# Values from three row tiles on, x of the second half loaded in one go, and mixed operands held in four PSUM banks, in a one-core encoder block

## What is computed

```python
h = rms_norm(x)
proj = h @ w_in            # lru_u | lru_y | q | k | v | gate_lru | gate_attn
lru_out = rg_lru(conv(lru_u)) * gelu(lru_y)       # 1280 channels, a scan over rows
attn_out = sliding_window_attention(q, k, v)      # 16 heads, 4 kv heads, 128 rows
mix = (g_lru * (lru_out @ w_lru_br) + g_attn * (attn_out @ w_attn_br)) @ w_out
x = x + rms_norm(mix)
h = rms_norm(x)
f = (silu(h @ w_ffn_gate) * (h @ w_ffn_up)) @ w_ffn_down
x = x + rms_norm(f)
```

## Time and profile before

| | |
|---|---|
| median of 3 runs | 1664.21 us (1663.47 to 1666.27) |
| the profiled execution | 1664.01 us, span 1662.2 us from first to last instruction |
| granted TensorE clock, mean | 0.99 of 2.4 GHz |
| PE busy | 1620.5 us, 97% of the span |
| POOL busy | 1231.1 us, 74% |
| DVE busy | 914.0 us, 55% |
| ACT busy | 571.3 us, 34% |
| moved by DMA | 187.88 MB, mean 113 GB/s |

### The profile page before, as it was taken

The page is one execution under the profiler, slowest core; times in us unless marked ns, Lnnn a source line. Parts: engine busy times, 40 slices in busy tenths (PEclk is TensorE's granted clock), DMA queues, the critical chain, the costliest instruction groups (busy, mean ns, idle before and its releaser), DMA issues.

```text
span 1662.2 us, 24258 instructions
## 1 busy us (share of the span) xinstructions
PE 1620.5 (97%) x7396; PEld 1337.0 (80%) x7396; DVE 914.0 (55%) x1160; ACT 571.3 (34%) x1073; POOL 1231.1 (74%) x1306
## 2 busy tenths in 40 slices
PE   8999999999999999999999998899999999999998
PEld 6788788888888888888878877688888888788887
DVE  5666536652265656666532457987775558415502
ACT  4588434532225776254422243310000113102101
POOL 5677767677786777777777876688887778768875
PEclk8999999999999999999999999999999999999999
DMA  4444433233354443522333564244432221633642
GB/s 149 121 114 115 111 97 90 80 92 95 95 146 123 115 120 99 163 81 74 89 95 95 147 218 154 75 121 115 114 95 64 68 76 57 236 97 95 221 121 86
DMA packets 119411, 187.88 MB, mean 113 GB/s; under 512 B 13345, under 2 KB 44321, under 8 KB 119329
## 3 DMA queue, kind: packets, MB, share of 16 engines
q1 hardware_dynamic: 95712, 143.18, 31.4%
q10 hardware_dynamic: 23616, 43.66, 8.0%
HBM read 162.93 MB, written 17.56 MB: 109 GB/s over the span
## 4 chain that ended last, share of the span: by engine, by line
PE 87%; DVE 6%; ACT 2%; issue 2%; DMA 1%; POOL 1%; ACTq 0%; DVEq 0%; POOLq 0%; SPq 0%
PE ps L818 14%; PE ps L819 14%; PE ps L817 14%; PE ps L1052 7%; PE ps L1054 7%; PE ps L1053 7%; PE ps L1146 4%; PE ps L1147 4%; PE ps L1148 4%; DMA xs<-x_t 1%; PE ps L871 1%; PE ps L872 1%; PE ps L873 1%; PE ps L888 1%; PE ps L967 1%
## 5 line engine op out<-in xcount | busy, mean ns | idle before, releaser
L660 POOL TENSOR_TENSOR w_lo<-w_raw,w_hi 128x512 fp32r<-128x512 f32 (+2 forms) x374 | 452.0, 1209 | 31.2
L657 POOL TENSOR_SCALAR w_hi<-w_raw 128x512 fp32r<-128x512 f32 (+2 forms) x374 | 240.2, 642 | 210.5 <-PE ps L819 130.0
L817 PE MATMUL ps<-h_hi,w_hi 128*128 128x512 f32 x672 | 263.7, 392 | 2.7 <-DVE g_h L1854 1.5
L818 PE MATMUL ps<-h_lo,w_hi 128*128 128x512 f32 x672 | 264.7, 394 | 0.0
L819 PE MATMUL ps<-h_hi,w_lo 128*128 128x512 f32 x672 | 264.1, 393 | 0.0
L817 PEld LDWEIGHTS ps<-h_hi,w_hi 128*128 128x128 f32 x672 | 126.5, 188 | 31.3 <-issue 1.8
L818 PEld LDWEIGHTS ps<-h_lo,w_hi 128*128 128x128 f32 x672 | 126.5, 188 | 27.2
L819 PEld LDWEIGHTS ps<-h_hi,w_lo 128*128 128x128 f32 x672 | 126.5, 188 | 27.2
L1798 DVE TENSOR_TENSOR acc<-acc,sq 128x512 f32<-128x512 f32 x47 | 49.3, 1049 | 175.3 <-ACT sq L1522 163.0
L1052 PE MATMUL ps<-t,w_hi 128*128 128x512 f32 x352 | 138.7, 394 | 1.4 <-POOL w_lo L710 1.4
L1054 PE MATMUL ps<-t,w_lo 128*128 128x512 f32 x352 | 138.0, 392 | 0.0
(11 more groups left out here) (363 smaller groups left out, 4054.0 us busy)
## 6 DMA issues: line engine op xcount, KB each, us to landing
w_raw<-w_f SPq DMA_DIRECT2D x68, 256.0 KB, 3.2
w_raw<-w_step SPq DMA_DIRECT2D x64, 256.0 KB, 2.7
w_raw<-w_b SPq DMA_DIRECT2D x64, 256.0 KB, 3.1
w_raw<-w_d SPq DMA_DIRECT2D x64, 256.0 KB, 2.7
w_raw<-w_a SPq DMA_DIRECT2D x96, 128.0 KB, 2.0
xs<-x_t ACTq DMA_DIRECT2D x32, 256.0 KB, 3.6
w_raw<-w_q SPq DMA_DIRECT2D x32, 256.0 KB, 3.1
w_raw<-w_o SPq DMA_DIRECT2D x32, 256.0 KB, 3.1
```

The lines of the kernel that those rows point to most:

```text
L657: nc.gpsimd.tensor_scalar(w_hi[:, s, w], w_raw[:, s, w], 1.0, 0.0, ALU.mult, ALU.add).then_inc(w_hi_made, 1)
L660: nc.gpsimd.tensor_tensor(w_lo[:, s, w], w_raw[:, s, w], rd(w_hi[:, s, w]), ALU.subtract).then_inc(w_lo_made, 1)
L817: mm(out, w_hi[:, s, w], x_hi, start=(k == 0), stop=False)
L818: mm(out, w_hi[:, s, w], x_lo, start=False, stop=False)
```

## The change

**Values.** PE waits for eight scans only and multiplies row tiles 0 to 2 with the first two weight blocks; then it waits for the ninth scan and multiplies row tile 3 with these two blocks, then all four tiles with blocks 2 and 3. The wait for the tenth scan moves behind the first tile of Q.

**x of the second half.** A buffer `x_next` of eight tiles lies on the place of b22. `between` of the second half issues its eight loads on ACT, after `normed_stream`. The loads in `x1_row` go, and `add_row` reads `x_next`; DVE waits once for all eight.

**Mixed operands.** Banks 4 to 7 (`BK_T`) take the first four tiles of h and then t1, the base of t2 and t4 in place; t3 and the last four tiles of h stay in SBUF. ACT copies t2's base to `rows` (`t2_keep`). The order on DVE and ACT is new, `stat_sum(5)` comes one pair of products earlier (t == 5), the weights of column tile 1 are loaded at t == 6 in place of t == 9, and `first_two` waits for each bank's low part of t4.

```diff
+        x_next = at("x_next", [P, KD, T], F32, reg_b + 4 * quad)
...
+        BK_INV, BK_ROW, BK_SQ, BK_T = 7, 5, (4, 6), (4, 5, 6, 7)
...
-                if t == 9:
+                if t == 6:
+                    sp_eng.wait_ge(normed, 3 * KD)
                     load_a21(1)
                     load_a12(1)
-                    sp_eng.wait_ge(added, 2 * KD)
                     load_a22(1)
                     load_a11(1)
...
+                pe.wait_ge(scanned, KR * h + 8)
+                pe.wait_ge(k_lo_made, PAIRS * h + 1)
+
+                def values(b, m):
...
+                for b in range(2):
+                    pe.wait_ge(w_lo_made, n_v + b + 1)
+                    for m in range(3):
+                        values(b, m)
                 pe.wait_ge(scanned, KR * h + 9)
-                pe.wait_ge(k_lo_made, PAIRS * h + 1)
-                for b in range(4):
+                for b in range(2):
+                    values(b, 3).then_inc(blocks_done, 1)
+                for b in range(2, 4):
                     pe.wait_ge(w_lo_made, n_v + b + 1)
...
+                    for m in range(3):
+                        values(b, m)
+                    values(b, 3).then_inc(blocks_done, 1)
...
+                project(0, n_q, 0, UNIT, h_hi, h_lo)
                 pe.wait_ge(scanned, KR * (h + 1))
-                for t in range(2):
-                    project(t, n_q + 2 * t, 2 * t, UNIT, h_hi, h_lo)
+                project(1, n_q + 2, 2, UNIT, h_hi, h_lo)
...
-                    if t == 6:
+                    if t == 5:
                         stat_sum(5)
...
-                    rows_out(n, o, 2, lambda: normed_stream(2, 3, x1_d[0]))
+
+                    def between():
+                        normed_stream(2, 3, x1_d[0])
+                        for c in range(KD):
+                            act.dma_start(x_next[:, c, :], x_d[1][c]).then_inc(x_next_loaded, 16)
+                    rows_out(n, o, 2, between)
...
+            def t2_keep(k):
+                act.wait_ge(t2_made, k + 1)
+                fn(rows[:, k, :], ps[:, BK_T[k], :], ACT.Copy).then_inc(t2_kept, 1)
...
-                dve.wait_ge(xs_loaded[c % 2], 16 * (4 * 4 + c // 2 + 1))
-                tt(rows[:, c, :], ps[:, 5, :], xs[:, c % 2, :], ALU.add).then_inc(added, 1)
+                tt(rows[:, c, :], ps[:, BK_ROW, :], x_next[:, c, :], ALU.add).then_inc(added, 1)
```

More of the change, by code:

```diff
@@ L919, in kvq @@
                 pe.wait_ge(dev_made, 3 if h else 1)
+                pe.wait_ge(scanned, KR * h + 8)
+                pe.wait_ge(k_lo_made, PAIRS * h + 1)
+                def values(b, m):
+                    out, t = ps[:, BK_V[m], 0:D_KV], slice(m * P, (m + 1) * P)
+                    for q in range(2):
+                        k, w = 2 * b + q, slice(q * D_KV, (q + 1) * D_KV)
+                        mm(out, h_hi[:, k, t], w_hi[:, b, w], start=(k == 0), stop=False)
+                        mm(out, h_lo[:, k, t], w_hi[:, b, w], start=False, stop=False)
+                        last = mm(out, h_hi[:, k, t], w_lo[:, b, w], start=False, stop=(k == KD - 1))
+                    return last
@@ L1661, in _ @@
             x1_row(1)
+            x1_row(2)
             first_copy(3)
-            x1_row(2)
+            x1_row(3)
             second_copy(2)
-            x1_row(3)
+            x1_row(4)
             first_copy(4)
-            x1_row(4)
+            x1_row(5)
+            x1_row(6)
             second_copy(3)
-            x1_row(5)
+            x1_row(7)
             first_copy(5)
-            x1_row(6)
+            acc_hi(5)
             second_copy(4)
-            x1_row(7)
-            acc_hi(5)
+            deviation(5)
             first_copy(6)
             second_copy(5)
-            deviation(5)
             first_copy(7)
+            for k in range(K2):
+                t_hi(h1_made, b22, rows[:, K2 + k, :], k)
             second_copy(6)
+            for k in range(K2):
+                t_hi(t3_made, t3, t3_f[:, 1, k, :], k)
             first_copy(8)
@@ L1682, in _ @@
             first_copy(9)
+            second_copy(8)
             for k in range(K2):
-                act.wait_ge(h1_made, k + 1)
-                fn(b22[:, 0, k, :], rows[:, K2 + k, :], ACT.Copy).then_inc(t_hi_made, 1)
-            second_copy(8)
+                t_hi(t1_made, t1, ps[:, BK_T[k], :], k)
             first_copy(10)
@@ L1699, in _ @@
             for k in range(K2):
-                t_hi(t2_made, t2, t4_f, k)
-            for k in range(K2):
-                t_hi(t4_made, t4, t4_f, k)
+                t_hi(t2_kept, t2, rows[:, k, :], k)
             for t in range(EARLY):
@@ L2245, in _ @@
             for k in range(K2):
-                dve.wait_ge(h1_made, K2 + k + 1)
-                tt(t3_f[:, 1, k, :], rows[:, K2 + k, :], rows[:, k, :], ALU.subtract).then_inc(t3_made, 1)
-            for k in range(K2):
                 dve.wait_ge(t3_made, k + 1)
@@ L2266, in _ @@
                 dve.wait_ge(t4_made, k + 1)
-                t_lo(4 * K2, t4, t4_f[:, 1, k, :], k)
+                t_lo(3 * K2, t4, ps[:, BK_T[k], :], k)
+            for k in range(K2):
+                t_lo(4 * K2, t2, rows[:, k, :], k)
             dve.wait_ge(copied, 2 * EARLY)
```

85 lines of the change are left out of this document (40 added, 45 removed).

## The result

| | before | after |
|---|---|---|
| median | 1663.84 us (4 runs) | 1653.03 us (1651.96 to 1654.18, 4 runs) |
| the profiled execution's span | 1662.2 us | 1651.4 us |
| granted TensorE clock, mean | 0.99 | 0.99 |
| busy PE / DVE / ACT / POOL, us | 1620.5 / 914.0 / 571.3 / 1231.1 | 1615.8 / 913.4 / 572.9 / 1231.3 |

A forecast was written before the change was run, and what follows sets the result against it. PE bounds the kernel (97% busy, 87% of the chain), so only its stalls and low clock can be saved. Gone 4.3 + 4.7 + 13.3 + 0.9 = 23.2, new 2.4 + 2.9 = 5.3: 1664.0 to 1646.2 us, range 1641 to 1654.

The forecast's parts named there:

- Values, 4.3 and 4.7: Starting Values before the ninth scan ends makes Q start 4.3 us earlier in the first half, 4.7 in the second.
- POOL's 0.9 wait: PE's first wait for POOL's w_lo, 0.9 us, after first_two goes because DVE is free earlier.
- Rival 4: Operations with a PSUM operand before first_two run slow beside POOL, 18 to 22 us more, at most 1668.3; chance 0.03.
- Rivals 3 and 5: 3: attention's chain sets the pace, early Values start lost, 1655.2, chance 0.05; 5: change does nothing, 1664.0, chance 0.03.
- Rival 2: Eight loads hold ACT 0.839 each, 1648.8; with low clock behind both new stalls, 1652.2; chance 0.09.
- The stall at `stat_sum(4)`, put at 2.4: x_next issues on ACT, 3.6 us, delay the second half's squares and adds by 2.7; less 0.3, a 2.4 us stall.
- The low clock at the new stalls: Clock drops behind the stalls at stat_sum(4) and S10: nothing in the sum, 2 x 1.7 us in rival 2.
- The stall at S10, put at 2.9: Second product of tile 10 waits for its bank, freed by ACT's copy behind t1's high part: 2.9 us.
- The Trainium skill's two rules in the prediction: DMA dispatch of 50 ns: no stat_sum(4) stall, time 2.4 lower; dearer PSUM operations: 0.065 each, time 0.8 more.
- The lower bound of the first stall: For the stall at stat_sum(4): issues of 8 x 0.357, by the earlier start, give 1.4 us.
- the reciprocal, b22 and the weight sums, 21 us: Part of DVE's 32 us chain before S10 said to keep its price, argued against the new stalls not showing.

The follow-up runs named there:

- run 1: Kernel before with only the new order of Values: 1651.89 us, ratio 0.9930.
- run 4: Changed kernel with the second half's output-projection squares kept in PSUM banks, so DVE's adds have a PSUM operand: 1649.51 us, ratio 0.9918.
- runs 5: Changed kernel with the eight x_next loads still issued on ACT, but earlier, ahead of the output projection: 1644.65 us, ratio 0.9894.
- run 8: Changed kernel with one DMA for all eight tiles of x_next, at the same place on ACT: 1644.72 us, ratio 0.9895.
- run 7: Changed kernel with the old order of Values restored: 1660.58 us, ratio 0.9996 to the kernel before.
- run 11: Kernel before with new Values, x_next issued early on ACT, mixes in SBUF, ACT's order changed and first_two starting with the last copy but one: 1643.30 us, ratio 0.9884.
- run 3: Changed kernel with ACT's copies of the early products put ahead of its high parts and t2-base copies: 1645.82 us, ratio 0.9896.
- 6 to 11: 6: edits of runs 5, run 3 and run 4 together, 0.9852; 9: run 1 plus early x_next, 0.9890; 10: edits of runs 5 and run 3, 0.9842.
- run 2: Changed kernel with the eight x_next loads issued by SP, ahead of the first early weight load: 1648.26 us, ratio 0.9909.

## Why the prediction was right and wrong

- **Values, 4.3 and 4.7:** right, 4.4 and 4.8 in the trace, the low clock behind the second hole gone with it; run 1 shows that it stands without the rest.
- **POOL's 0.9 wait gone:** right by the earlier trace rows against the waits of after, where 0.5 is left.
- **Rival 4, slow operations in banks:** dead; the mixes with a bank take 0.6 to 0.7 each. Rivals 3 and 5 too. Rival 2's 1652.2 is the number nearest to the measured 1653.03, and half its mechanism held: a low clock came with each new stall. Its other half did not: ACT was held 4.72 us, not 6.7. It is so near partly by luck.
- **The stall at `stat_sum(4)`, put at 2.4, was 7.0: the first of two steps that failed, 4.6 us.** It has two errors. I took the median issue, 454 ns, times eight. The median here is 454 again, but one of the eight took 1391, and the sum was 4.72 for 3.6; a run of in-line issues costs its mean. The larger error, 3.4 us, is the sentence "From there on the tiles are one chain of square and add, so all come 2.7 later". The chain did not move rigidly: moved by a few us it came to lie beside POOL's splits, where an add took 1.5 to 1.8 us for 0.7. The sign stood in the rows: rival 4 quoted 1.44 to 1.61 for operations within SBUF beside POOL; I weighed that for the mixes and not for the adds. The Trainium skill states the mechanism in "SBUF — State Buffer", SBUF: two separate sides: a VectorE operation with two SBUF inputs and a GpSimd operation that reads SBUF lock each other out for a whole instruction. The trace agrees: the adds at 951.89 and 954.58 end 0.55 us after the `w_lo` at 951.82 and 954.57 do, and the adds with a bank (run 4) do not see POOL at all.
- **The low clock at the new stalls, put at nothing in the sum, was 4.9: the second step that failed.** It stood only in rival 2, with 2 x 1.7 and a chance of 0.09. It came, with 1.9 and 3.0. Each stall was priced as its own length, and a hole of 4.2 us cost 7.2 with its clock. The sign was in the trace of before: at its own hole of 4.6 us in this stretch the clock was low for 6.8 us, part of the 0.96 in the earlier trace rows.

```profile
1004.80:1011.60 6.80, 4.28 (x10) 3.43 (x11) 5.55 (x7) 2.62 (x5) 0.03 (x1) 0.50 0.77 242
```

- **The stall at S10, put at 2.9:** mechanism and place right, size small: 4.2, and 5.1 in runs 5 and 8, where nothing holds PE back ahead of it. It is DVE's weight sums, four operations, reckoned at 0.69 each, 2.8, which is what they took before, with POOL idle. In the changed kernel they took 4.1, the 1.3 that the stall is longer. In run 8:

```profile
984.07 1.78 DVE L2138 TENSOR_TENSOR s_sum<-w_raw 128x512 f32<-128x512 f32 x1
985.95 0.92 DVE L2143 TENSOR_TENSOR s_sum<-s_sum,w_raw 128x512 f32<-128x512 f32 x1
986.79 1.79 DVE L2144 TENSOR_TENSOR w_raw<-w_raw 128x512 f32<-128x512 f32 x1
988.69 0.91 DVE L2149 TENSOR_TENSOR w_raw<-w_raw,s_sum 128x512 f32<-128x512 f32 x1
989.53 3.35 DVE L2224 RECIPROCAL ps<-rstd_b 128x512 f32<-128x512 f32 x1
...
1016.42 2.48 DVE L2275 TENSOR_TENSOR ps<-ps,t_f 128x512 f32<-128x512 f32 x4
```

They take 5.46, 2.7 more. The rest of the chain up to the last t1 takes 29.4 where 29.3 was reckoned, by errors that cancel (b22's and t3's low parts 10.4 for 9.2, the tiles of h, t3 and t1 shorter). The weight sums too read SBUF only, beside POOL: the same error as above.

- **The Trainium skill's two rules in the prediction.** "DMA: Bandwidth & Descriptors", Anatomy of one DMA, gives 50 ns of dispatch, in the breakdown of a DMA that GpSimd issues; here ACT issues, and it took 0.39 us for the one issue and 0.59 in the mean of eight. "Issuing engines are not separate DMA queues" calls it small relative to the DMA itself: that agrees, 5.9 us in the median from issue to landing, but ACT stood for all eight. "VectorE: DVE Perf Modes", The TRN2 errata, gives 62 cycles more for a PSUM source: the same add takes 0.69 within SBUF where POOL is idle (run 8) and 0.69 with a bank (run 4), so no such cost shows.

- **Small slips in the working.** The lower bound of the first stall is 1.2 and not 1.4 (956.0 + 2.9 + 1.6 against 958.98, less 0.3); "the reciprocal, b22 and the weight sums, 21 us" is 16 without t3's low parts. Neither moves the forecast.

The sum closes on the two profiles. The changed kernel is ahead of the kernel before by 0.5 us at Values of the first half, by 4.9 behind it, 6.6 at Values of the second half, 11.4 behind it, 8.2 at `first_two`, 9.2 behind the wait for POOL that is gone, and 10.8 from about 1420 us on. Values gave 9.2, the stretch around the two new stalls took 3.3, POOL's wait gave 0.9 to 1.0: the edits made 6.9. The forecast of 17.9 less the misses (4.6 and 1.3 for the stalls, 1.9 and 3.0 for the clock) and with the 0.2 more of Values is 7.3. The other 3.8 of the 10.8 (0.5, 1.7 and 1.6) came at places that no edit touches; two of them are described in the last section. So it is partly luck that the time still lies at the upper edge of the range of 1641 to 1654. By the medians the parts are less sharp: run 7 puts all but Values between 2.2 us gained and 0.8 lost, where the profiles have 2.4 lost.

## What to carry to other kernels

DMAs issued in line on ACT cost it about half a microsecond each here (0.59 in the mean of eight tiles, 0.39 for one DMA of all eight), by the issue and not by the byte; join loads that are needed together into one DMA, or issue them where the engine waits anyway, and early enough not to meet transfers that are due. When a chain of short operations is moved, look at what will then run beside it: here a shift of under 4 us became 7 because VectorE's adds with both inputs in SBUF took twice as long beside GpSimd's splits. A stall that is added needs its low clock in the sum: here 1.9 and 3.0 on top of 7.0 and 4.2. On an engine in order, the copy that frees a bank goes ahead of the operation whose input is not yet made; that order, and not the length of the mixes, decided whether the banks paid.

## What was not expected of the hardware

**PE's pace has spells.** In full clock and without waits, PE's matmuls of 512 columns start 0.229 us apart nearly everywhere. In the profiled execution of the kernel before they start 0.2333 apart over a whole stretch. The first and last of 236 records there, then of 241 records of the changed kernel in the same stretch of time:

```profile
569.98 0.40 PE L818 MATMUL ps<-h_lo,w_hi 128*128 128x512 f32 x1
...
624.81 0.40 PE L819 MATMUL ps<-h_hi,w_lo 128*128 128x512 f32 x1
```
```profile
570.04 0.39 PE L819 MATMUL ps<-h_hi,w_hi 128*128 128x512 f32 x1
...
624.98 0.39 PE L819 MATMUL ps<-h_hi,w_hi 128*128 128x512 f32 x1
```

54.83 us for 235 steps against 54.94 for 240, both at a granted clock of 1.00. Over 555 to 645 us it makes 1.7 us between the two profiles that no edit made. Such spells came at other places too (25 to 60 us in the kernel before and in run 11, 190 to 235 in run 3, 970 to 995 in the changed kernel), and what starts them was not found.

**The low clock does not follow every hole.** The same hole of 2.5 us near 66 us was followed by 3.4 us at 1.2 GHz in the kernel before and in runs 4 and 5, and by none in the changed kernel and in runs 1, 3 and 6 to 11 (in run 2 it came 8 us earlier, behind a hole of 1.8); the hole of 1.9 near 1410 likewise was followed by a low clock in the kernel before and in runs 2, 4, 5 and 8, and by none in the changed kernel and in the other runs. Each is worth 1.7 us. The length differs as well: waits of 4.1 to 4.9 us at S10 go with 6.8 us of low clock in the changed kernel and in run 7 and with 3.4 in runs 2, 4, 5 and 8. Two profiles thus differ by some us before any edit does, and a reckoning by their rows has to leave these places out before it is set against the medians.
